# The experts' down rows issued from SP's queue between the gate and up columns, instead of from GpSimd's queue

## What is computed

```
logits = x @ w_router + b_router
top_w  = softmax of the two largest logits of a token
for e in range(8):
    out += gate[..., e] * ((silu(x @ w_gate[e]) * (x @ w_up[e])) @ w_down[e])
```

## Time and profile before

| | |
|---|---|
| median of 3 runs | 2615.14 us (2611.57 to 2618.77) |
| the profiled execution | 2602.88 us |
| its span, first to last instruction | 2601.1 us |
| TensorE busy | 2352.4 us, 90% of the span |
| VectorE busy | 1633.4 us, 63% |
| ScalarE busy | 1195.7 us, 46% |
| GpSimd busy | 295.3 us, 11% |
| read from main memory | 439.10 MB |
| granted TensorE clock, mean | 0.925 |

### The profile page before, as it was taken

How to read it: one execution, slowest core, us unless ns; L and a number is a source line. 1 busy time by engine, 2 the same in 40 slices (tenths; PEclk the granted TensorE clock), 3 DMA queues, 4 the chain that set the end, 5 groups by cost and what they waited for, 6 DMA issues and landing times.

```text
span 2601.1 us, 30795 instructions
## 1 busy us (share of the span) xinstructions
PE 2352.4 (90%) x12628; PEld 2018.7 (78%) x12628; DVE 1633.4 (63%) x1903; ACT 1195.7 (46%) x1338; POOL 295.3 (11%) x305
## 2 busy tenths in 40 slices
PE   7899959889989998899958889789999999999995
PEld 6788737589989997887736789778888788787884
DVE  5755525566544436675435666467878878878783
ACT  4444313143344326354213243256666666666663
POOL 1321021200000002230122100000000000000000
PEclk9999758899999999999659899889999999999998
DMA  6232340744445453233241734459998999889981
GB/s 162 76 93 82 109 131 17 226 122 129 137 129 146 125 132 90 82 94 93 81 135 60 222 104 138 139 188 335 338 336 307 354 324 341 322 316 342 329 306 54
DMA packets 434604, 471.12 MB, mean 181 GB/s; under 512 B 17674, under 2 KB 319002, under 8 KB 434456
## 3 DMA queue, kind: packets, MB, share of 16 engines
q1 hardware_dynamic: 389052, 349.51, 42.9%
q0 software_dynamic: 26240, 100.67, 10.6%
q10 hardware_dynamic: 19164, 18.88, 2.1%
HBM read 439.10 MB, written 29.92 MB: 180 GB/s over the span
## 4 chain that ended last, share of the span: by engine, by line
PE 72%; DVE 12%; ACT 6%; DMA 4%; issue 2%; SPq 2%; POOL 1%; ACTq 0%; DVEq 0%; POOLq 0%
PE bank L880 9%; PE bank L912 8%; PE bank L914 8%; PE bank L913 8%; PE bank L557 7%; PE bank L558 7%; PE bank L559 7%; PE bank L816 2%; DVE arena L1712 2%; PE bank L658 2%; DVE weight_parts L1666 2%; DMA weights<-in_w_ex_gate 2%; PE bank L924 2%; ACT weight_parts L1175 1%; PE bank L718 1%
## 5 line engine op out<-in xcount | busy, mean ns | idle before, releaser
L1803 DVE TENSOR_TENSOR w_rest<-weights,w_high 128x2048 fp32r<-128x2048 f32 x176 | 394.9, 2285 | 15.8 <-ACT w_high L1297 15.8
L1297 ACT ACTIVATE w_high<-weights 128x2048 fp32r<-128x2048 f32 x176 | 326.5, 1905 | 35.4 <-DMA weights<-in_w_ex_gate 21.3
L1666 DVE TENSOR_TENSOR weight_parts<-weights,weight_parts 128x1024 fp32r<-128x1024 f32 x192 | 239.6, 1259 | 121.1 <-ACT weight_parts L1175 110.9
L1175 ACT ACTIVATE weight_parts<-weights 128x1024 fp32r<-128x1024 f32 x192 | 201.2, 1054 | 220.3 <-PE bank L559 109.0
L557 PE MATMUL bank<-x_high,weight_parts 128*128 128x320 f32 x896 | 288.3, 322 | 6.5 <-DVE x_rest L1690 6.4
L912 PE MATMUL bank<-w_high,tokens_high 128*128 128x512 f32 x704 | 279.9, 398 | 6.6 <-issue 3.2
L558 PE MATMUL bank<-x_high,weight_parts 128*128 128x320 f32 x896 | 282.0, 315 | 0.0
L559 PE MATMUL bank<-x_rest,weight_parts 128*128 128x320 f32 x896 | 281.5, 314 | 0.0
L914 PE MATMUL bank<-w_high,tokens_rest 128*128 128x512 f32 x704 | 277.3, 394 | 0.0
L913 PE MATMUL bank<-w_rest,tokens_high 128*128 128x512 f32 x704 | 275.4, 391 | 0.0
L1809 DVE TENSOR_TENSOR w_rest<-weights,w_high 128x2048 fp32r<-128x2048 f32 x88 | 201.6, 2291 | 93.5 <-ACT w_high L1305 93.4
(11 more groups left out here) (406 smaller groups left out, 4825.2 us busy)
## 6 DMA issues: line engine op xcount, KB each, us to landing
weights<-in_w_ex_gate SPq DMA_DIRECT2D x88, 1024.0 KB, 7.2
weights<-in_w_ex_up SPq DMA_DIRECT2D x88, 1024.0 KB, 7.5
weights<-in_w_ex_down POOLq DMA_DIRECT2D x88, 1024.0 KB, 7.2
weights<-in_w_in SPq DMA_DIRECT2D x144, 512.0 KB, 3.8
weights<-in_state_mlstm_c SPq DMA_DIRECT2D x32, 512.0 KB, 7.7
out_c_sample<-weights ACTq DMA_DIRECT2D x32, 512.0 KB, 5.3
weights<-in_w_ff_gate SPq DMA_DIRECT2D x22, 512.0 KB, 4.0
weights<-in_w_ff_up SPq DMA_DIRECT2D x22, 512.0 KB, 5.2
```

The costliest lines, as they stand in the source:

```text
L1175: nc.scalar.activation(parts[s], raw_of(*item), ACT.Copy).then_inc(*ac_s.done("weights high", *item))
L1297: nc.scalar.activation(w1h[s][:, k], mo_w1[s][:, k], ACT.Copy).then_inc(mo_w1h[s], 1)
L1666: nc.vector.tensor_tensor(parts[RAW[item][0]], raw_of(*item), parts[HIGH[item][0]], ALU.subtract)\
L1803: nc.vector.tensor_tensor(w1l[s][:, k], mo_w1[s][:, k], w1h[s][:, k], ALU.subtract)\
```

## The change

Issuing the down rows moves from GpSimd's stream into SP's loop. SP's loop now runs 90 times: in turn q it waits for the columns buffer and issues columns(q), as before, and then, from q = 2 on, waits for the down buffer and issues down(q-2) with the same semaphores and the same DMA; the last two turns issue down rows alone. GpSimd's `experts`, its repeat for crowded experts and the semaphore `mo_room` go away. The waits for the four last ring buffers move from GpSimd to SP, ahead of SP's first columns. The DMAs, their sizes, buffers and the work of the other engines stay as they are.

```diff
--- before.py
+++ after.py
@@ -471,9 +471,8 @@
             for n in ("columns_landed", "down_landed", "columns_high", "columns_rest", "down_high", "down_rest",
                       "selection_made", "gates_selected", "gathered", "gate_up_done", "silu_done", "hidden_done", "hidden_turned",
                       "hidden_high", "hidden_rest", "down_done")]
-        mo_xh, mo_xg, mo_ys, mo_sc, mo_acc, mo_shift, mo_room, mo_a, mo_v = [
+        mo_xh, mo_xg, mo_ys, mo_sc, mo_acc, mo_shift, mo_a, mo_v = [
             sem(f"moe_{n}") for n in ("tokens_high", "tokens_in_sbuf", "outputs_in_sbuf", "scattered", "added", "shifted",
-                                      "down_room_seen",
                                       "scalar_steps", "vector_steps")]
         ENG = {"pe": pe_s, "act": ac_s, "dve": dv_s, "pool": po_s}
 
@@ -2320,29 +2319,12 @@
                 pool.wait_ge(*pe_s.at("mm", l, "gb", 1, 3))
                 nc.gpsimd.tensor_tensor(x1T, xl, xh, ALU.add).then_inc(*po_s.done("x again", l))
 
-            def experts(ps):
-                for p in range(STEPS):
-                    e, j = divmod(p, EST)
-                    pool.wait_ge(mo_w2l[p % 2], 44 * ps + p // 2 + 1)
-                    if not isinstance(ps, int):
-                        pool.sem_inc(mo_room, 1)
-                    pool.dma_start(mo_w2[p % 2], I["w_ex_down"][0, e, j * NG:(j + 1) * NG, :]
-                                   .rearrange("(f p) n -> p f n", p=P)).then_inc(moe_in2[p % 2], 16)
-
-            for s in range(8, SLOTS):
-                vacated(pool, FINAL[1][s])
             pool.wait_ge(*pe_s.at("var1", 1))
             nc.gpsimd.memset(tri8, 1.0).then_inc(*po_s.done())
             pool.wait_ge(*po_s.last())
             nc.gpsimd.affine_select(out=tri8, in_=tri8, compare_op=ALU.is_gt, fill=0.0, base=0,
                                     pattern=[[1, NE], [-1, NE]], channel_multiplier=0).then_inc(*po_s.done("tri8"))
             nc.gpsimd.iota(iotaI, pattern=[[1, P]], base=0, channel_multiplier=0).then_inc(*po_s.done("moe"))
-            experts(0)
-            pool.wait_ge(*dv_s.at("pos"))
-            flag = pool.value_load(over, min_val=0, max_val=1)
-            with pool.If(flag > 0):
-                with pool.Fori(1, 3) as ps:
-                    experts(ps)
 
 
         @block.sync
@@ -2370,7 +2352,17 @@
                 sp.dma_start(dst, source_of(l, name, i, j)).then_inc(ring_full[s], 16)
 
             def experts(ps):
-                for q in range(STEPS):
+
+                def down_rows(p):
+                    e, j = divmod(p, EST)
+                    sp.wait_ge(mo_w2l[p % 2], 44 * ps + p // 2 + 1)
+                    sp.dma_start(mo_w2[p % 2], I["w_ex_down"][0, e, j * NG:(j + 1) * NG, :]
+                                 .rearrange("(f p) n -> p f n", p=P)).then_inc(moe_in2[p % 2], 16)
+
+                for q in range(STEPS + 2):
+                    if q >= STEPS:
+                        down_rows(q - 2)
+                        continue
                     s = q % 2
                     e, ch, kind = step_of(q)
                     n0 = 512 * (ch % CHUNKS)
@@ -2385,6 +2377,8 @@
                             sp.dma_start(mo_w1[s][:, 4 * i:4 * i + 4],
                                          w[0, e, 512 * i:512 * i + 512, n0:n0 + 512].rearrange("(k p) n -> p k n", p=P))\
                                 .then_inc(moe_in[s], 16)
+                    if q >= 2:
+                        down_rows(q - 2)
 
             def load_down(j):
                 sp.dma_start(ff_w2[j % 3], I["w_ff_down"][0].rearrange("(f p) (i n) -> p i f n", p=P, n=P)[:, j])\
@@ -2458,7 +2452,7 @@
                         sp.wait_ge(*(pe_s.at("ff up", FC - 1) if j == 2 else pe_s.at("ff down", j - 3)))
                         load_down(j)
                 else:
-                    for s in range(8):
+                    for s in range(SLOTS):
                         vacated(sp, FINAL[l][s])
                     experts(0)
                     sp.wait_ge(*dv_s.at("pos"))
```

## The result

The changed kernel takes 2774.24 us (median of 4 runs, 2767.09 to 2776.13), against 2613.36 us (2609.47 to 2618.77, 4 runs) for the kernel before beside it: +161 us, a ratio of 1.0615 with a 95% interval of 1.0592 to 1.0638. The forecast was 2745 with a range of 2690 to 2785. The profiled execution took 2767.09 us, its span is 2765.3 us. Every line number of the changed kernel from the gather on is one less than before; VectorE's down_rest is L1808, columns_rest L1802, ScalarE's rounding of columns L1296, and on SP the down rows are L2359 and the columns L2377.

What follows compares the result with a forecast made beforehand. TensorE was taken to bound the expert stage, DMA close behind. Late loads +109 us and clock +28 made +137, giving 2740 on the profiled execution or 2752 on the median; it said 2745, range 2690 to 2785.

Steps and rivals of the forecast that it cites:

- What bounds, and the order: Expert stage: TensorE sets the pace, 5.2 us idle; on one queue every columns load waits behind a later release.
- The landing: SP's queue: down and two columns megabytes in a row land 10.5 us after down's issue; bounds 7.8 and 11.7.
- The loop: Plain expert steps: from burst issue to the next release 20.0 us for two steps, 10.0 a step against about 9.
- The sum over an expert: Eleven steps of 10.0 us plus gather 5.5 and scatter 4.5: 120.0 against 105.1, +15 an expert, +109 us in all.
- the gather's example: Step 44: columns wait behind a down release that comes only after the gather, so TensorE's product is 5.1 us late.
- The clock: TensorE's clock falls after waits at gathers and scatters: 14 waits at 2.0 us, +28 us, range 0 to 41.
- What costs nothing: Stage start, SP's 88 added issues and GpSimd's lost ones cost nothing; the end gains at most 0.4 us.
- A: Rival, same time: bursts land within 8.4 us of down's release, so nothing is lost; 2603 to 2615 us, chance 0.05.
- B: Rival, faster: GpSimd's path slowed down loads or columns, one queue lands columns sooner; 2598 to 2610 us, chance 0.02.
- D: Rival: the long gather and scatter steps hide the loop; +35 to +80, 2640 to 2690 us, chance 0.06.
- C: Rival: the loop's loss without the clock, TensorE staying at 2.4 GHz; +109, 2712 to 2724 us, chance 0.25.
- E: Rival: slow landing of 11.7 us, +162 and up to some 25 of clock; 2765 to 2800 us, chance 0.10.

Runs made afterwards that it cites:

- one columns load earlier: Changed kernel with each down load on SP's queue one columns load earlier, down(q-1) behind columns(q): 3550.39 us, one run.
- the added wait: Kernel before, down rows on GpSimd's queue, but SP waits before columns(q) for the release that down(q-3) needs: 2769.04 us, ratio 1.0587 to the kernel before.
- the third order: Changed kernel with each down load on SP's queue one columns load later, down(q-3) behind columns(q): 2605.07 us, ratio 0.9955 to the kernel before.
- the fill: Changed kernel with matmuls whose result nothing reads put into TensorE's long waits, before experts' first columns and in scatters: 2746.53 us, ratio 1.0496 to the kernel before.
- the run with 64 KB: Changed kernel loading only 64 KB of each 1 MB down block from the third down load on, waits and order kept: 2690.29 us, ratio 1.0298 to the kernel before.

## Why the forecast was right, and where it was off

**What bounds, and the order.** Right. The three traces with SP held back (the changed kernel, one columns load earlier, the added wait) show it: TensorE idle, ScalarE waiting for columns, SP released by down_rest but for the stage's start. The cause is the place in the order: the third order has the queue without the loss, the added wait has the loss without the queue.

**The landing.** 10.5 us was taken, between 10.4 and 11.1. Over the 83 bursts of the stage the last megabyte lands 10.9 us after down's issue (median, 10.2 to 12.4); in the plain step above it is 10.3. Two things go with a late landing. One is a burst still under way when the next leaves. The other the forecast did not have: DMA packets of the queue that the profile calls instruction, 28 of 16 KB each in the stage. Of the 40 bursts whose predecessor had landed, the 15 with such a packet between issue and landing took 11.6 us (median), the 25 without 10.4. The gather's burst of 2192.71 is one with a packet, as the view of 2192.7 to 2204.4 us has it (packets, MB, share of the engines):

```profile
q8 instruction: 1, 0.02, 0.9%
```

No run was made that moves these packets, so that they are the cause is not shown. Medians over the stage:

```profile
weights<-in_w_ex_down SPq DMA_DIRECT2D x79, 1024.0 KB, 5.0
weights<-in_w_ex_up SPq DMA_DIRECT2D x79, 1024.0 KB, 9.4
weights<-in_w_ex_gate SPq DMA_DIRECT2D x79, 1024.0 KB, 9.0
```

The down rows themselves land sooner than from GpSimd (5.0 us against 7.4), being first in line; the price is paid by the columns, whose medians were 7.2 and 7.5 before.

**The loop.** 20.0 us was worked out; 19.6 was read off above, and 19.5 to 20.0 where it spans a single step. The term is right. That it stretches all eleven steps to 10.0 is not what happened: steps 1, 5 and 9 stayed at 8.3 to 8.5 us.

**The sum over an expert is the step that was mis-sized.** The forecast took 11 x 10.0 + 5.5 + 4.5 = 120.0 us. The kernel with its waits filled, near to the forecast's case without the clock, takes 122.9 from gather to gather, the changed kernel 126.4. So the 109 us were about 161 - 28 = 133, if the fill gives back all that the clock costs. The forecast had the gather's example at 5.1 us late; step 10 lost 6.2. In the example above the columns landed after 11.7 us and not 10.5, though the burst before had landed 4.4 us before this one left. And the scatter's step lost 5.9 us, of which 30.8 / 7 = 4.4 are its wait for VectorE's adds, where the forecast had set down a price for the clock but no time for the wait itself. Adding the loop and the long steps was still right in kind: neither hides the other, as 84 + 39 show. But the forecast spread its 15 us over eleven steps of 10.0, and the table has most of them behind the gather and at the scatter, so that the expert's sum came this near is in part luck.

**The clock.** 28 us forecast, 27.7 got back by the fill. That agreement is in part luck: it counted 14 waits at 2.0 us, while the filled kernel still has a clock of 0.98, so a part of the clock's price is still in it, and the added matmuls are not known to be free.

**What costs nothing.** Right: the stage's first columns left at 1671.6 us, 1 us later than before, and the tail is unchanged.

**The rivals.** A (cover holds) falls: the burst never landed within 8.4 us. Its point of 8.4 us held for the plain steps 5 to 7 in the run with 64 KB, and not for the steps after the gather and up to the scatter. What A draws from the Trainium skill (DMA: Bandwidth & Descriptors, Issuing engines are not separate DMA queues) is the wrong way round: the section says that issuing on several engines saves issue time, so by it the move to one queue could cost some and not save it. No run here shows such a cost: the third order was not slower. B (GpSimd's path as brake) may be true in small, and only in another order: with down rows behind the columns that the release order puts there, 7 to 12 us are won; which part of the path is at work is open. In the Trainium skill, SBUF — State Buffer (section SBUF: two separate sides) gives a GpSimd starved by VectorE's 2-port operations as a reason for SP's queue; no run here shows that. D (long steps hide the loop) is the reverse of what was found: the waits stand at the long steps. C is nearest to the fill. E's span of time, 2765 to 2800, holds the measured 2774, and its landing of 11.7 us was reached by a part of the bursts only.

## What to carry to other kernels

Before loads of two kinds are put on one queue, write down for each the instruction that frees its buffer, and put the loads in the order in which those instructions run; a load ahead of its turn holds all behind it. A load that comes late feeds the instruction that releases a later load, so add the loop up, from issue over landing and conversion to the next release, and divide by the steps it spans: under the bound engine's step it costs nothing, above it every step. Long steps with their own late releases, and the clock of TensorE after a wait, come on top.

## What had not been expected

Useless matmuls made a kernel faster: 224 of them took 27.7 us off. And two queues were not quite as good as one in the right order: in the repeated trace of the kernel before a columns megabyte took up to 14.9 us to land, in that of the third order up to 10.9, and this order was 0.3 to 0.5% faster than the kernel before in 19 runs of two kernels.
